# The last chunk of each output projection multiplied bank by bank, and the state-space norm taken by group

## The reference, cut to what matters

```
h = layer_norm(DN_ALPHA * h + g1 * mixer(u), ln1_g, ln1_b)     # mixer ends in ... @ w_out
h = layer_norm(DN_ALPHA * h + g2 * swiglu(u), ln2_g, ln2_b)    # swiglu ends in ... @ w2
```

```
h = rms_norm(x, norm1_w)
z, xbc, dt_raw, q, k, v = split(h @ w_in)
xbc = silu(depthwise_conv(xbc)); y_ssm = ssd(forward) + ssd(backward) + d_skip * xs      # 16 heads of 64
y_ssm = y_ssm * silu(z)                           # in 2 groups of 512 features
y_ssm = rms_norm(y_ssm, ssm_norm_w)               # a mean square per group
x = x + concat(y_ssm, windowed_attention(q, k, v)) @ w_out
h = rms_norm(x, norm2_w); g, u = split(h @ w_up)
x = x + (silu(depthwise_conv(g)) * u) @ w_down    # and after both layers rms_norm(x, final_norm_w)
```

## Time and profile before

| what | before |
|---|---|
| median of 3 runs | 2222.73 us (2218.28 to 2227.9) |
| the profiled execution, its own time | 2226.38 us |
| its span, first to last instruction | 2224.6 us |
| granted TensorE clock, mean | 0.967 of full speed |
| busy: TensorE, VectorE, ScalarE | 2045.8, 1521.2, 995.0 us |
| HBM read | 355.41 MB |

### The profile page before, as it was taken

The page is one execution under the profiler, slowest core; times in us unless marked ns, Lnnn a source line. Parts: engine busy times, 40 slices in busy tenths (PEclk is TensorE's granted clock), DMA queues, the critical chain, the costliest instruction groups (busy, mean ns, idle before and its releaser), DMA issues.

```text
span 2224.6 us, 37066 instructions
## 1 busy us (share of the span) xinstructions
PE 2045.8 (92%) x15578; PEld 1918.0 (86%) x15578; DVE 1521.2 (68%) x2756; ACT 995.0 (45%) x1437; POOL 22.2 (1%) x36
## 2 busy tenths in 40 slices
PE   5899999999988989999999889987999989897998
PEld 4898889999988988889899778776999878687998
DVE  7887576677668876766755478765666588655665
ACT  3553454344445544553544324444444334444444
POOL 2000000000010000000000000000000000000000
PEclk8999999999999999999999999999999999899999
DMA  8455444457644554345555343221555242123552
GB/s 316 152 190 192 168 150 154 171 212 279 240 153 141 201 195 171 130 158 186 195 206 188 111 171 132 77 77 61 196 188 190 100 137 106 58 95 114 193 198 102
DMA packets 52770, 358.98 MB, mean 161 GB/s; under 512 B 5995, under 2 KB 8651, under 8 KB 9980
## 3 DMA queue, kind: packets, MB, share of 16 engines
q1 hardware_dynamic: 52412, 356.51, 44.9%
q10 hardware_dynamic: 192, 0.10, 0.0%
HBM read 355.41 MB, written 1.08 MB: 160 GB/s over the span
## 4 chain that ended last, share of the span: by engine, by line
PE 79%; DVE 14%; ACT 4%; issue 1%; DMA 1%; SPq 0%; ACTq 0%; DVEq 0%
PE projected L427 31%; PE projected L1414 20%; PE mixed L427 7%; PE mixed L1414 5%; DVE cacc L1794 3%; PE mixed L1589 2%; DVE w_lo L352 1%; PE mixed L1508 1%; PE mixed L501 1%; DVE nrm L941 1%; PE mixed L479 1%; PE mixed L561 1%; PE mixed L1497 1%; PE mixed L1520 1%; PE mixed L488 1%
## 5 line engine op out<-in xcount | busy, mean ns | idle before, releaser
L352 DVE TENSOR_TENSOR w_lo<-raw,w_hi 128x1024 fp32r<-128x1024 f32 x340 | 409.4, 1226 | 232.0 <-ACT w_hi L646 230.4
L646 ACT ACTIVATE w_hi<-raw 128x1024 fp32r<-128x1024 f32 x338 | 350.6, 1055 | 376.3 <-PE projected L427 310.7
L427 PE MATMUL projected<-u_hi,w_hi 128*128 128x256 f32 x1728 | 489.9, 284 | 25.5 <-DVE u_lo L852 25.5
L427 PE MATMUL projected<-u_lo,w_hi 128*128 128x256 f32 x1728 | 484.6, 280 | 0.0
L427 PE MATMUL projected<-u_hi,w_lo 128*128 128x256 f32 x1728 | 484.2, 280 | 0.0
L427 PEld LDWEIGHTS projected<-u_hi,w_hi 128*128 128x128 f32 x1728 | 329.9, 191 | 32.6 <-issue 32.1
L1352 DVE TENSOR_TENSOR w_lo<-raw,w_hi 128x1024 fp32r<-128x1024 f32 x204 | 245.9, 1223 | 153.6 <-ACT w_hi L1648 153.4
L427 PEld LDWEIGHTS projected<-u_lo,w_hi 128*128 128x128 f32 x1728 | 329.5, 191 | 0.2
L427 PEld LDWEIGHTS projected<-u_hi,w_lo 128*128 128x128 f32 x1728 | 327.8, 190 | 0.0
L1414 PE MATMUL projected<-u_hi,w_hi 128*128 128x256 f32 x992 | 282.1, 284 | 32.1 <-DVE w_lo L1352 32.1
L1648 ACT ACTIVATE w_hi<-raw 128x1024 fp32r<-128x1024 f32 x204 | 210.9, 1054 | 158.9 <-PE projected L1414 140.6
(11 more groups left out here) (361 smaller groups left out, 4100.9 us busy)
## 6 DMA issues: line engine op xcount, KB each, us to landing
raw<-in_stream_dram SPq DMA_DIRECT2D x324, 1024.0 KB, 4.9
w_mod<-in_first_ada_dram SPq DMA_DIRECT2D x8, 1024.0 KB, 15.1
band<-bias_rows SPq DMA_DIRECT2D x1, 3072.0 KB, 14.6
x<-in_xT_dram SPq DMA_DIRECT2D x1, 1024.0 KB, 4.9
out_dram<-uf SPq DMA_DIRECT2D x4, 256.0 KB, 2.5
tri<-in_tri_dram SPq DMA_DIRECT2D x2, 384.0 KB, 4.1
c<-in_c_dram SPq DMA_DIRECT2D x1, 512.0 KB
mask<-in_mask_dram SPq DMA_DIRECT2D x1, 384.0 KB, 25.5
```

The source lines that it names most:

```text
L352: eng.tensor_tensor(part(w_lo, step, half), raw_half(step, half), part(w_hi, step, half).bitcast(F32), ALU.subtract).then_inc(s_lo_dve, 1)
L427: m = pe.matmul(out, a, b, start=start and n == 0, stop=stop and n == 2, **kw)
L646: act.activation(part(w_hi, step, half), raw_half(step, half), ACT.Copy).then_inc(s_hi, 1)
```

## The change

1. In w2 (first stack), wo2 and wd (second stack) the last chunk runs bank by bank: both input tiles for bank 0, then for bank 1, and so on. A semaphore (s_bank) tells of each finished bank, and VectorE's residual and ScalarE's squares follow each. The two increments of the weights' semaphore come together at the end.
2. The column sums (first stack) and the sums of squares (second stack) are spread: two tiles at a time, after later chunks of wo, and after banks 2 and 3 of w2, wo2 and wd. The sums take a bank of their own (PB in rotation, or MB[0]).
3. In the state-space stage the four z projections come first. Gate and square of a pair follow that pair's yT within the ssd step. The norm is taken by group: group 0 after ssd step 11, group 1 after attention step 1. The first wo2 chunk follows group 1's sum; WO_AFTER is shifted accordingly. y_hi and y_lo lie where zs and yT lay. The table load stands in group 0's norm.

The core of the diff (semaphore numbers, tables of names and the closing norm's ScalarE part are left out):

```
+        def sum_features(l, i, first):
+            for kt in range(first, first + 2):
+                pe.wait_ge(s_pre, 16 * l + 8 * i + kt + 1)
+                m = pe.matmul(NB[i][0][:, 0:T], ones_d[:], hT[:, kt, :], start=kt == 0, stop=kt == KT - 1)
+            return m
...
                 project(step, (mix_hi, mix_lo), {0: (s_ml, 3 * l + 1), 4: (s_ml, 3 * l + 2), 6: (s_ml, 3 * l + 3)})
+                if i:
+                    sum_features(l, 0, 2 * i - 2)
             elif kind == "ln":
-                for kt in range(KT):
-                    pe.wait_ge(s_pre, 8 * N + kt + 1)
-                    m = pe.matmul(NB[i][0][:, 0:T], ones_d[:], hT[:, kt, :], start=kt == 0, stop=kt == KT - 1)
-                m.then_inc(s_mean, 1)
+                if i == 1:
+                    sum_features(l, 1, 4)
+                sum_features(l, i, 6).then_inc(s_mean, 1)
...
+                parts = [split(step, kt) for kt in range(2)] if i == FP - 1 else ()
+                for b in range(4) if i == FP - 1 else ():
+                    for n in (2 * b, 2 * b + 1):
+                        for kt, (hi, lo) in enumerate(parts):
+                            m = product(MB[b][:, n % 2 * T:(n % 2 + 1) * T],
+                                        (hi[:, n * P:(n + 1) * P], lo[:, n * P:(n + 1) * P]),
+                                        (hid_hi[:, 2 * i + kt, :], hid_lo[:, 2 * i + kt, :]), False, kt == 1,
+                                        skip_group_check=True)
+                    if b < 3:
+                        m.then_inc(s_bank, 1)
+                    else:
+                        m.then_inc(s_used, 2)
+                    if b >= 2:
+                        sum_features(l, 1, 2 * b - 4)
+                for kt in range(2) if i < FP - 1 else ():
...
-                    dve.wait_ge(s_used, done(("w2", FP * l + FP - 1)))
                     for kt in range(KT):
+                        if kt == 6:
+                            dve.wait_ge(s_used, done(("w2", FP * l + FP - 1)))
+                        elif kt % 2 == 0:
+                            dve.wait_ge(s_bank, 3 * l + kt // 2 + 1)
...
-WO_AFTER = (3, 5, 7, 9, 11, 13, 16, SH + VALUES - 1)
+WO_AFTER = (1, 3, 5, 7, 9, 12, 15, SH + VALUES - 1)
...
     ssd = [("x_turn", i) for i in range(4)] + [("ssd", i) for i in range(SH + VALUES)]
-    plan += interleave([("ak2", 0), ("av2", 0)] + [("aq2", i) for i in range(4)] + [("z", i) for i in range(4)], ssd)
-    plan += [("ssd_gate", 0), ("att2", 0), ("att2", 1), ("ssd_norm", 0)]
+    plan += interleave([("z", i) for i in range(4)] + [("ak2", 0), ("av2", 0)] + [("aq2", i) for i in range(4)], ssd)
+    plan.insert(plan.index(("ssd", 11)) + 1, ("group_norm", 0))
+    plan += [("att2", 0), ("att2", 1), ("group_norm", 1), ("wo2", 0)]
...
-    y_hi = place("y_hi", [P, KT, T], 10, F32R)
-    y_lo = place("y_lo", [P, KT, T], 18, F32R)
+    y_hi = place("y_hi", [P, KT, T], 58, F32R)
+    y_lo = place("y_lo", [P, KT, T], 50, F32R)
...
+        def accumulate_last(step, banks, x, tile, norm):
+
+            sums = bank(("rms", norm)) if norm % 2 == 0 else MB[0]
+            parts = [split(step, kt) for kt in range(2)]
+            for b in range(4):
+                for n in (2 * b, 2 * b + 1):
+                    for kt, (hi, lo) in enumerate(parts):
+                        m = product(banks[b][:, n % 2 * T:(n % 2 + 1) * T],
+                                    (hi[:, n * P:(n + 1) * P], lo[:, n * P:(n + 1) * P]),
+                                    (x[0][:, tile + kt, :], x[1][:, tile + kt, :]), False, kt == 1, skip_group_check=True)
+                if b < 3:
+                    m.then_inc(s_bank, 1)
+                else:
+                    m.then_inc(s_used, 2)
+                if b >= 2:
+                    sum_squares(sums, norm, b - 2)
+
+        def sum_squares(out, norm, pair):
+            pe.wait_ge(s_sq, 4 * (norm - 1) + pair + 1)
+            for kt in range(2 * pair, 2 * pair + 2):
+                m = pe.matmul(out[:, 0:T], ones_d[:], sqn[:, kt, :], start=kt == 0, stop=kt == KT - 1)
+            return m
...
+            if n == 0:
+                pe.wait_ge(s_yrs, SG * l + SG)
...
-                for kt in range(KT):
-                    if N == 0:
+                if N == 0:
+                    out = bank(step)
+                    for kt in range(KT):
                         pe.wait_ge(s_sq0, kt + 1)
-                    elif kt % 2 == 0:
-                        pe.wait_ge(s_sq, 4 * (N - 1) + kt // 2 + 1)
-                    m = pe.matmul(MB[0][:, 0:T], ones_d[:], sqn[:, kt, :], start=kt == 0, stop=kt == KT - 1)
+                        m = pe.matmul(out[:, 0:T], ones_d[:], sqn[:, kt, :], start=kt == 0, stop=kt == KT - 1)
+                else:
+                    out = PB[turn(step)] if i == 0 else MB[0]
+                    for pair in (2, 3):
+                        m = sum_squares(out, N, pair)
                 m.then_inc(s_var, 1)
...
-            elif kind == "ssd_norm":
-                pe.wait_ge(s_ysq, l + 1)
-                if l == 0:
+            elif kind == "group_norm":
+                out = bank(step) if i == 0 else MB[2]
+                pe.wait_ge(s_ysq, 4 * N + 4)
+                if N == 0:
                     pe.wait_ge(s_const, 5)
-                for g in range(SG):
-                    for n in range(4):
-                        m = pe.matmul(PB[0][:, g * T:(g + 1) * T], ones_g[:], sq[:, 4 * g + n, :],
-                                      start=n == 0, stop=n == 3)
+                for n in range(4):
+                    m = pe.matmul(out[:, 0:T], ones_g[:], sq[:, 4 * i + n, :], start=n == 0, stop=n == 3)
                 m.then_inc(s_yvar, 1)
...
-                if i in (0, 2):
-                    pe.wait_ge(s_yn, 2 * l + i // 2 + 1)
+                if i < 4:
+                    pe.wait_ge(s_yn, 4 * l + i + 1)
                 if i >= 4:
                     pe.wait_ge(s_o, ENDS["o"] + KT * l + 2 * (i - 4) + 2)
-                accumulate(step, PB, (y_hi, y_lo) if i < 4 else (o_hi, o_lo), 2 * (i % 4), i == 0, i == 7)
+                if i == 7:
+                    accumulate_last(step, PB, (o_hi, o_lo), 2 * (i % 4), 2 * l + 1)
+                else:
+                    accumulate(step, PB, (y_hi, y_lo) if i < 4 else (o_hi, o_lo), 2 * (i % 4), i == 0, False)
...
                 b = result(step)
+                if i < 2:
+                    act.wait_ge(s_xbc, 6 * l + 6)
...
+                if i > VALUES and i % 2 == 0:
+                    pair = (i - 4) // 2
+                    act.wait_ge(s_yg, KT * l + pair + 1)
+                    act.activation(sq[:, pair, :], yT[:, pair, :], ACT.Square).then_inc(s_ysq, 1)
+            elif kind == "group_norm":
+                act.wait_ge(s_yvar, N + 1)
+                if i == 0:
+                    act.preload_act_table_set(LOG_EXP)
+                out = PB[turn(step)] if i == 0 else MB[2]
+                link(act.activation(grs[:, i, :], out[:, 0:T], ACT.Ln, bias=eps[:, 0:1]))
+                act.activation(grs[:, i, :], grs[:, i, :], ACT.Exp, scale=-0.5).then_inc(s_yrs, 1)
                 for n in range(2):
-                    act.wait_ge(s_yf, 2 * l + n + 1)
-                    act.activation(y_hi[:, 4 * n:4 * n + 4, :], yT[:, 4 * n:4 * n + 4, :], ACT.Copy)\
-                       .then_inc(s_yh, 1)
+                    pair = slice(4 * i + 2 * n, 4 * i + 2 * n + 2)
+                    act.wait_ge(s_yf, 2 * N + n + 1)
+                    act.activation(y_hi[:, pair, :], yT[:, pair, :], ACT.Copy).then_inc(s_yh, 1)
...
+                    dve.wait_ge(s_yT, KT * l + pair + 1)
+                    dve.wait_ge(s_zs, 4 * l + pair // 2 + 1)
+                    dve.scalar_tensor_tensor(out=yT[:, pair, :], in0=zs[:, pair, :], scalar=0.5, in1=yT[:, pair, :],
+                                             op0=ALU.mult, op1=ALU.mult).then_inc(s_yg, 1)
+            elif kind == "group_norm":
+                dve.wait_ge(s_yg, 4 * N + 4)
+                dve.wait_ge(s_yrs, N + 1)
                 for n in range(2):
-                    for kt in range(4 * n, 4 * n + 4):
+                    for kt in range(4 * i + 2 * n, 4 * i + 2 * n + 2):
                         ins = dve.scalar_tensor_tensor(out=yT[:, kt, :], in0=yT[:, kt, :], scalar=column(l, V2_SN + kt),
-                                                       in1=grs[:, n, :], op0=ALU.mult, op1=ALU.mult)
+                                                       in1=grs[:, i, :], op0=ALU.mult, op1=ALU.mult)
                     ins.then_inc(s_yf, 1)
                 for n in range(2):
-                    quad = slice(4 * n, 4 * n + 4)
-                    dve.wait_ge(s_yh, 2 * l + n + 1)
-                    dve.tensor_tensor(y_lo[:, quad, :], yT[:, quad, :], y_hi[:, quad, :].bitcast(F32),
+                    pair = slice(4 * i + 2 * n, 4 * i + 2 * n + 2)
+                    dve.wait_ge(s_yh, 2 * N + n + 1)
```

(23 more changed lines are left out.)

32 lines of the change are left out of this document (9 added, 23 removed).

## The result

| | before | after |
|---|---|---|
| median, 5 runs of each | 2218.28 us (2217.32 to 2227.9) | 2182.27 us (2173.57 to 2196.37) |
| the profiled execution's span | 2224.6 us | 2194.6 us |
| granted TensorE clock, mean | 0.967 | 0.970 |

The ratio is 0.9831, 95% interval 0.9802 to 0.986: the medians lie 36 us apart (31 to 44 by the interval), 1.7%. I had forecast 2195.1 and a range from 2186 to 2207. The profiled execution is the slowest of the five, and against that of before it won only 30.0 us, near my 27.6. So there are two things to explain: what the change won beyond the sum, and why executions of one kernel lie 23 us apart.

A forecast was written before the change was run, and what follows sets the result against it. TensorE, busy 92% of the span, was taken as the bound, so only its waits and slow clock after them could be won. -21.6 - 5.8 - 1.2 + 1.0 = -27.6 us took the 2222.7 median to 2195.1, range 2186 to 2207.

The forecast's parts named there:

- The end of the state-space stage: Last projection through first output chunk, attention steps 2 and 3 now included: 33.4 us becomes 18.0, 15.4 removed per layer.
- Group 0's sum: Added among the heads after head step 11: 1.9 us of work and 1.7 of waiting, 3.6 us per layer.
- Rival 2: Squares among the exponentials reload tables, about 2.6 us per layer: 2200, up to 2206; chance 0.04.
- z first: State-space stage: zs 2 and 3 fall on the first heads, where VectorE is late; 1.0 us added per layer.
- Bank by bank: Last chunks: waits of 1.44 us at four second-block norms go, -5.8 us; first block's w2 -1.2 us.
- The first block's 1.2 us: w2's last chunk bank by bank: the residual's wait of 0.6 us goes, twice, -1.2 us.
- Switches: Ten more changes from a sum back to a split product, taken at 0.1 us each: +1.0 us (0 to 4).
- one wait of about 1 us at head step 4: Sign expected in the changed profile among the state-space heads, where z first was charged 1.0 us per layer.
- Rival 1: The norm in the middle of the heads holds TensorE, 4 to 6 us per layer: 2205; chance 0.12.
- Rival 3: Attention bound by its own chain: uncovered third steps and undrained queues cost 9 us per layer, 2213; chance 0.05.
- Rival 4: Slower: weights come late in every head group, ScalarE's rounding standing behind a square; 2234; chance 0.03.
- Rival 5: More is won: no wait at group 0's sum, z free, no switch cost; 2187; chance 0.06.

The follow-up runs named there:

- z_first_alone: The kernel before, with only the four z projections put in front of k, v and q beside the heads; 2214.44 us, ratio 0.998.
- keys_first: The changed kernel with k and v projected first, then the four z, then q; 2193.73 us, ratio 0.9889.
- kick_short: The changed kernel with one extra 128-column matmul in front of each gate projection but the first, in all four feed-forward stages; 2196.7 us.

## Why the prediction was off

Measured in the second block at equal pace the change is worth 939.9 - 907.3 = 32.6 us. Of my 27.6, 26.4 belonged to this block. (The 939.9 is one profile; the other two of before, less 7.1 for their slow stage, give 940.5 and 940.0.) So 6 us were missing in the sum. Of the 12.8 by which the forecast missed, another 4.4 are the level from which I started, and the last 2 lie within the spread of executions. That the profiled pair lies only 30.0 apart, near my 27.6, was luck and bears nothing out.

- **The end of the state-space stage: right.** 33.4 to 18.0 forecast, 17.8 measured. Scores began 3.8 us after the last projection, not 4.35. Group 1's sum took 1.99 (1.9). Chunk 0 took 6.0 (5.7), steps 2 and 3 with the start of the next chunk 5.2 (4.9).
- **Group 0's sum: right.** Wait 1.75 and work 1.97, 3.7 us, against 1.7 and 1.9. In the row of the waits one layer's is put down to the square, the other's to "issue": the chain in the timeline is the same in both. ScalarE's rows:

```profile
1405.93 0.42 ACT L1797 ACTIVATE sq<-yT 128x256 f32<-128x256 f32 x1 [0.87 <-DVE yT L1988]
1407.23 0.84 ACT L1793 ACTIVATE W<-W 128x768 f32<-128x768 f32 x1 [0.89 <-DVE W L1973]
1408.44 1.28 ACT L1801 ACT_TABLE_LOAD   x1 [0.36 <-PE projected L1655]
1409.73 0.47 ACT L1803 ACTIVATE grs<-projected,eps 128x256 f32<-128x256 f32 x1
```

  No table load stands around the square; the only one comes before Ln, hidden under a projection. Rival 2 did not happen: an exponential follows the square directly. The Trainium skill (ScalarE: Activation LUTs, "Table sets: the hidden batching unit") tells to batch calls by set; the square did not count as another set here, and the load measures 1.28 us, with Ln right behind it, not the about 2.7 that the Trainium skill gives there.
- **z first: the step that failed.** My sum had "1.0 us added" per layer, from what zs 2 and 3 bring onto VectorE at the heads. That part is there: E-H is up by 4.6, of which group 0's sum is 3.7, and 0.6 of the rest is the wait at head 2. But I weighed only what z brings to its new place and never asked what it replaces there, although the row of the wait, 1.39 us, was in the trace. In the old order v is the second projection; it needs both halves of its weights, waits 1.39 us for them, and its products then ran partly at the granted clock of 0.50. H-P went from a mean of 24.2 (22.8 to 25.8) to 21.8. Net 1.5 won where 1.0 was charged: 5 us over two layers. z_first_alone and keys_first show the order's effect from both sides; that v and not k's copies is behind it is read from the times of the rounding, not from a run that moves v alone.
- **G-E** fell by 16.9; by my terms (15.4, 1.44, less 0.4 for switches) by 16.4. The 0.5 is the earlier start of the scores, which z first also brings: before, the last z's multiplication (0.69 us) stood in VectorE's queue ahead of the last head's mask, and with a q projection last nothing does. 1 us over two layers.
- **Bank by bank: right.** 6.8 forecast, 6.6 measured alone (2 to 11 by the interval). The feed-forward stages with their norms are 0.9 and 1.6 us shorter at equal pace, 2.5 against 2.9. The first block's 1.2 us can't be seen: its waits are gone from the rows, and its length varies by 14 us.
- **Switches:** charged with 1.0 us, and no row shows them apart. Of the 0.4 us that bounded one (5.86 against 5.45) half is no switch but the two paces: 48 x 4.5 ns = 0.2.
- **The level and the range.** I started from 2222.7, a median of three runs. Of the five sets of before in the record, the result's, which holds those three runs, has 2218.3, and the four later ones have medians from 2214.7 to 2215.5. Against 2218.28 my own 27.6 gives 2190.7, inside the range. And its lower end was a sum with everything won, 2186, with nothing for the spread of executions: I had spent that on the upper end alone. A range drawn from one profile for a kernel whose executions lie 20 us apart needed 10 us on either side.

The sign "one wait of about 1 us at head step 4" came as 0.6 at head 2. Rival 1's delay at the group's sum stayed at the 1.75 us in the sum. Rival 3's third uncovered attention step cost what I took: from the end of one chunk (1485.72 + 5.45) to the next (1499.65) are 8.5 us where two steps take 5.8, so 2.7. Rival 4 did not come near. Rival 5 named z free and more won, with 2187 and a chance of 0.06; it was the one that came closest.

## What to carry to other kernels

When a step is moved, ask what each step in the new order needs before it can start: a projection that takes its weights by halves begins 1.1 us earlier in a place where they come just in time than one that wants both. The cost at the new place is half of the account. A row with a wait of 1.4 us twice in the trace is worth looking up even when the edit seems to be about something else, and its cause is whatever ended just before the wait did: here the copies that I suspected began only after the rounding in question was over. And before comparing two kernels by a few us, take the same kernel's profile more than once. H-P, E-H and G-E repeated here within 0.4 us in the changed kernel while whole executions differed by 23, so the stage table finds in a few profiles what five timed rounds can't; in the kernel before H-P moved by 3.

## What the chip did that I had not expected

TensorE's stream of 128x256 matmuls, each with its weight load, has two paces at full granted clock, 113.3 and 117.8 ns. A pace held through whole feed-forward stages, 180 us and 1584 matmuls, and in kick_short one added matmul of 128 columns turned it into the other each time. The Trainium skill (TensorE: Matmul & The Clock Gate, "Back-to-back issue gap") gives 2.5 ns above the columns at 2.4 GHz, as the gap of matmuls without the weight loads between them, from which an estimate for 256 columns is 109 ns; both paces measured here, with weight loads, are slower. Which stage gets which pace changed from execution to execution of the same kernel, and with it the time by 7 us a stage. The cause stays open.
